# Hybrid Mamba-2 / pooling / mixture-of-experts block on one core: the table transfers of token blocks 1 to 3 wait for the mixer's last product

## What is computed

```python
x = x + (g_ssd * y_ssd + g_pool * y_pool) @ w_mix_out[i]
h = rms_norm(x, ffn_norm_g[i])
...
logits = (hf @ w_router + b_router).astype(jnp.float32)
top_val, top_idx = lax.top_k(logits, TOP_K)
weights = jax.nn.softmax(top_val, axis=-1)
...
xb = hf[tok]
gu = xb @ w_gate_up[e] + b_gate_up[e]
gate, up = jnp.split(gu, 2, axis=-1)
...
act = (up + 1.0) * gate * jax.nn.sigmoid(SWIGLU_ALPHA * gate)
return act @ w_down[e] + b_down[e]
```

## Time and profile before

| what | value |
|---|---|
| median of 3 runs | 1843.52 us |
| the profiled execution's own time | 1857.41 us |
| span in the profile, first to last instruction | 1855.6 us |
| PE busy | 1808.1 us (97%) |
| DVE busy | 1411.4 us (76%) |
| ACT busy | 1179.0 us (64%) |
| POOL busy | 363.7 us (20%) |
| mean granted clock of TensorE | 0.991 |
| mixer, up to the slot transfers | 0 to about 617 us of the span |
| experts, steady | about 675 to 1770 us of the span |

### The profile page before, as it was taken

One profiled execution on the slowest core, in us unless ns is written; L12 is line 12 of the kernel. 1 busy time (PEld: TensorE's weight loads), 2 busy tenths in 40 slices (PEclk: granted clock), 3 DMA queues, 4 the chain that ended last, 5 costly groups with the idle time before them and its releaser, 6 DMA issues.

```text
span 1855.6 us, 25522 instructions
## 1 busy us (share of the span) xinstructions
PE 1808.1 (97%) x8997; PEld 1501.0 (81%) x8997; DVE 1411.4 (76%) x1027; ACT 1179.0 (64%) x936; POOL 363.7 (20%) x324
## 2 busy tenths in 40 slices
PE   7999999999999799999999999999999999999997
PEld 6888888678889778888888888888888888888876
DVE  4576676553334489989998988988988988989974
ACT  5655565342232367777777777777777777777774
POOL 5223324520000321211221221111111211121000
PEclk9999999999999899999999999999999999999999
DMA  6434443343346189999999999999999999999941
GB/s 184 131 96 103 115 133 99 103 142 91 92 140 258 58 326 372 368 369 379 370 374 373 375 368 383 370 374 385 375 368 377 376 373 374 376 371 368 380 162 46
DMA packets 153769, 504.50 MB, mean 272 GB/s; under 512 B 15691, under 2 KB 76147, under 8 KB 120085
## 3 DMA queue, kind: packets, MB, share of 16 engines
q1 hardware_dynamic: 141684, 478.50, 68.9%
q0 software_dynamic: 11984, 25.22, 5.8%
q10 hardware_dynamic: 48, 0.07, 0.0%
HBM read 493.67 MB, written 26.30 MB: 280 GB/s over the span
## 4 chain that ended last, share of the span: by engine, by line
PE 84%; DVE 5%; ACT 3%; POOL 3%; issue 3%; DMA 1%; another core or an unknown queue 1%; SPq 0%; DVEq 0%; POOLq 0%; ACTq 0%
PE gu_ps L2112 25%; PE gu_ps L2116 12%; PE dn_ps L2127 12%; PE gu_ps L1880 7%; PE gu_ps L1882 7%; PE gu_ps L1881 7%; PE dn_ps L2133 6%; PE et_ps L2098 3%; ACT w_hi L911 1%; PE dn_ps L2283 1%; PE gu_ps L1902 1%; POOL win L814 1%; POOL dx L800 1%; PE gu_ps L2283 1%; PE gu_ps L2104 1%
## 5 line engine op out<-in xcount | busy, mean ns | idle before, releaser
L1696 DVE TENSOR_TENSOR split_l<-ring,split_h 128x2048 fp32r<-128x2048 f32 x384 | 870.1, 2292 | 94.2 <-ACT split_h L1177 91.2
L1177 ACT ACTIVATE split_h<-ring 128x2048 fp32r<-128x2048 f32 x384 | 728.9, 1916 | 145.9 <-PE gu_ps L2116 114.2
L2112 PE MATMUL gu_ps<-split_h,xgT_h 128*128 128x512 f32 x992 | 272.9, 397 | 1.5 <-DVE xgT_l L1702 1.5
L2112 PE MATMUL gu_ps<-split_h,xgT_l 128*128 128x512 f32 x992 | 266.9, 391 | 0.0
L2116 PE MATMUL gu_ps<-split_l,xgT_h 128*128 128x512 f32 x992 | 266.8, 391 | 0.0
L2116 PEld LDWEIGHTS gu_ps<-split_l,xgT_h 128*128 128x128 f32 x992 | 186.8, 188 | 40.1
L2112 PEld LDWEIGHTS gu_ps<-split_h,xgT_l 128*128 128x128 f32 x992 | 186.6, 188 | 40.1
L2112 PEld LDWEIGHTS gu_ps<-split_h,xgT_h 128*128 128x128 f32 x992 | 181.6, 188 | 43.4 <-issue 8.6
L1356 DVE TENSOR_TENSOR w_lo<-w_raw,w_hi 128x2048 fp32r<-128x2048 f32 (+1 forms) x45 | 102.8, 2285 | 143.2 <-ACT w_hi L911 130.8
L827 POOL COPY icur<-slots 128x1 int32 (+1 forms) x31 | 50.6, 1631 | 670.3 <-PE et_ps L2098 670.3
L2127 PE MATMUL dn_ps<-split_h,actT_h 128*128 128x512 f32 x496 | 155.4, 394 | 0.0
(11 more groups left out here) (358 smaller groups left out, 2625.3 us busy)
## 6 DMA issues: line engine op xcount, KB each, us to landing
ring<-in_w_gate_up SPq DMA_DIRECT2D x256, 1024.0 KB, 7.2
ring<-in_w_down SPq DMA_DIRECT2D x128, 1024.0 KB, 7.9
w_raw<-in_w_in SPq DMA_DIRECT2D x28, 1024.0 KB, 5.9
arow<-acum_rows POOLq DMA_DIRECT2D x16, 512.0 KB, 6.5
w_raw<-in_w_ssd_out SPq DMA_DIRECT2D x8, 1024.0 KB, 6.1
w_raw<-in_w_in SPq DMA_DIRECT2D x9, 512.0 KB, 6.4
w_raw<-in_w_mix_out SPq DMA_DIRECT2D x4, 1024.0 KB, 8.8
wpg<-in_w_ple_gate SPq DMA_DIRECT2D x2, 2048.0 KB, 20.1
```

The costliest lines, as they stand in the source:

```text
L1177: a.activation(split_h[s % SPLIT][:, :], ring[s % RING][:, :], ACT.Copy).then_inc(hi_done, 1)
L1696: v.tensor_tensor(split_l[s % SPLIT][:, :], ring[s % RING][:, :], split_h[s % SPLIT][:, :].bitcast(F32), ALU.subtract).then_inc(lo_done, 1)
L2112: t.matmul(gu_ps[:, b * 512:b * 512 + 512], x[:, k, :], split_h[s][:, b * 512:b * 512 + 512], start=False, stop=False)
```

## The change

After `send(0)`, GpSimd waits until VectorE has read the last product of the mixer's output, `MO(3, 1)`, and only then goes on to `send(1)`, `send(2)` and `send(3)`. Nothing else is touched.

```diff
             pool.wait_ge(filled, 16 * PASSES + 16)
-            for c in range(CH):
+            send(0)
+            wait_proj_read(pool, ("MO", CH - 1, 1))
+            for c in range(1, CH):
                 send(c)
             pool.wait_ge(rows_stored, 16 * CH)
             step(g.memset(xg[:, :], 0.0))
```

## The result

The changed kernel takes 1850.73 us (median of 6 runs, 1849.1 to 1851.91); the kernel before took 1843.32 us beside it (6 runs, 1841.73 to 1845.19). The ratio is 1.0038, with a 95% interval of 1.0028 to 1.0048: slower by 7.4 us. The forecast was 1848.3, slower by 4.8.

What follows compares the result with a forecast made beforehand. PE was taken to bound the expert stage, so a delayed start delays the end. With no stall in timed runs, 4.8 us of late transfers added to 1843.5 gave 1848.3 us; range 1835.0 to 1851.5.

Steps and rivals of the forecast that it cites:

- the forecast's case: Seam before the experts: timed runs have no stall, the hold only makes slot transfers late, 4.8 us slower; chance 0.50.
- the transfer that was to be held by the norm: POOL's block 1 and 2 transfers after the wait: one of the eight was expected to be held by VectorE's norm.
- The page rule that I weighed against the trace: Descriptor generation not seen to stall under tensor_tensor; by it the change costs the wait's 3.1 us alone, 1846.6 us.
- the sum: All lateness at the seam reaches the end and nothing later wins it back: 1843.5 + 4.8 = 1848.3 us.
- the 4.8: Lateness in us of SP's weight issue from the wait and transfers held by splits; estimates 3.7 to 7.2, mostly 4.8.
- the prediction's own baseline: Kernel before rebuilt without the stall: last row_idx 632.6, SP's weights 644.7, 1857.4 less 11.8 giving 1845.6 us.
- The reading that fell: Residual add's 9.8 us stall before the router belongs to the profiled execution, not the timed runs; held at 7 in 10.
- The gap: Profiled time less median, 13.9 us before; shrinking to 2 us in the changed kernel would confirm the no-stall reading.
- The first rival: The residual add's stall is in every run and the hold removes it: 7.0 us gained, 1836.5 us; chance 0.30.
- Its point of decision: The first rival decides if the residual add's stall in timed runs is over 4.8 us long.
- D: Expectation in the experiments: chips differ in speed alone, whatever the kernel, so the ratio is 1.004 everywhere.
- C: Expectation in the experiments: the stall belongs to a chip; ratio 0.9975 where the kernel before stands near 1855, 1.004 near 1843.

Runs made afterwards that it cites:

- e3: Kernel before with blocks 1 to 3 held until VectorE has written the last normed block (h2_done = 4): 1855.15 us, ratio 0.9996.
- e2: Kernel before with the same wait placed only ahead of send(3), where it is already met: 1855.42 us, ratio 1.0001.
- e5: The changed kernel, unchanged, beside the kernel before on the second chip: 1847.99 us, ratio 0.9974.
- e4: Kernel before without a hold, plus four more indirect transfers of block 2 into a spare table ahead of block 3: 1859.07 us, ratio 1.0026.
- e9: The kernel before, unchanged, profiled again on the third chip: 1856.15 us, ratio 1.0003.
- e7: Kernel before, with SP issuing the first expert's chunks 6 and 7 before it waits for the slot transfers: 1854.76 us, ratio 1.0007.
- e11: Kernel before, with GpSimd gathering before it weighs and SP issuing the second expert's first two chunks ahead of the biases: 1855.15 us, ratio 1.0.
- e1: The kernel before, unchanged, profiled once more on the first chip: 1854.01 us, ratio 0.9999.
- e10: The changed kernel, unchanged, on the third chip: 1848.83 us, ratio 0.9961 against the kernel before.
- e6: Kernel before with the wait placed ahead of block 2, so that block 1 goes unheld: 1850.89 us, ratio 0.9984.
- e8: Changed kernel, with SP issuing the first expert's chunks 6 and 7 before it waits for the slot transfers: 1850.72 us, ratio 0.9986 against the kernel before.

## Why the prediction was right, and where it was not

**The sign and the mechanism.** In the first comparison it went as the forecast's case said, step by step: the wait costs 2.8 us at block 1 (626.75 against 623.9, where an unheld one would follow the fourth, issued at 622.63; predicted 3.1), the add is free, `row_idx` comes 8.0 us behind the start of the add (8.1, counted from 624.5), SP issues 15.6 us after it (15 to 18), and the second expert begins at 668.72 (near 669). That delay passes on undiminished to the second expert is shown by e3. That a wait which delays nothing costs nothing is shown by e2. One small step was wrong: the transfer that was to be held by the norm is free (628.03, 0.97 us, with the norm at 627.96).

The page rule that I weighed against the trace, the Trainium skill, "SBUF — State Buffer", section "Who interferes with whom" (descriptor generation not seen to stall under tensor_tensor), does not fit this trace: four transfers of 1.90 to 2.93 us stand beside such splits, and the 1846.6 us that would follow from the rule are too few. The measurement decides.

**The size.** The term that was mis-sized is what stands behind the seam, which the sum took as untouched: "Nothing later wins it back, since PE bounds the experts". Nothing wins it back, but something adds to it. The late chunks make PE pause, and in this profile the granted clock falls behind the pause; later the second expert's first products run in half clock. In 10 of the 14 profiles the time from PE's start on that expert to its activation is about 23.1 us, in e5 for one, with the clock full. In the changed kernel's it is 25.6. So the clock takes about 2.6 us there, in this execution. If the timed runs of the kernel before lose nothing at that place, the sum is 4.8 + 2.6 = 7.4, which is what was measured. That it meets the number exactly is luck: the 4.8 is an estimate, and by the prediction's own baseline (SP at 644.7, so the second expert at 663.4) the second expert comes 5.3 us late. The same correction mends the baseline. I rebuilt it from the profile at 1845.6, and that profile carries a loss of its own there (24.7 against 23.1, 1.6 us); without it the baseline is 1844.0, within 0.7 of the 1843.3 that was timed. That the kernel before runs with the clock full there when nothing stalls is argued, not shown: no profile of it without the stall exists. e3, the other seam without a stall at the add, shows the loss as well (24.7 us), with its pauses still longer. But e4 and the first profile of the kernel before, which do stall, show 24.7 too, and e9, the same kernel as the latter, 23.1. So the cause of this loss is not settled, nor is it shown for each timed run: of the changed kernel's 6, four have the profile's mean granted clock of 0.994, and the two fastest, 1849.1 and 1849.92 us, have 0.995 and 0.996.

**The reading that fell.** I put the stall down to the profiled execution, at 7 in 10, because the profile was 13.9 us above the median. Outside the first comparison the runs speak against it: the kernel before stalls in both later profiles (9.10 and 9.08) and in those of its variants without a hold (9.05 in e2, 5.37 in e7, 9.07 in e11), profiled and other runs agree (1852.9 and 1854.0; 1857.7 and 1856.2), and the levels are those of a kernel with the stall. On the second chip the kernel before itself was timed but not profiled. By the Trainium skill, "NOTIFIC — the notification-queue block", section "7.1 Overflow: three behaviours, one of which stalls the engine", the stall could have been the profiler's. e1 and e9 do not bear that out, since the profiled run costs nothing extra there, but they don't rule it out either: every execution of the later groups, and every one of the changed kernel in the first comparison, has its span and granted clock on record, and so was recorded in some way, while the 6 executions of the kernel before at 1843.3 have only their times there. Recording alone does not bring the delay, though: the changed kernel's first profile has none. The step that failed is "So the likeliest reading is that the runs that are timed don't have this stall". It may hold for the first comparison, but one profile, of an execution that is none of the timed ones, was thin ground for it. The gap did shrink to under 2 us, as the reading asked, but it would have done so in any kernel whose add doesn't stall; that sign could not tell the readings apart.

**The first rival** was right in its sign wherever the runs have the stall: 5.1 us gained on the second chip and 7.0 on the third, against 7.0 worked out. Its point of decision, a stall of over 4.8 us, fits too: it is 9.1 us in the profiles of the first and third chip. That its price was met is luck. It had the last `row_idx` 12.4 us earlier and SP's issue 5.4 us further behind it. From block 2's `row_idx` to the last one it is 19.9 us in e9 and 13.3 in e10, so 6.5 us were won, since a wait of 5.38 us came up at the ranks; and SP issues 11.9 us behind the last `row_idx` in both, so nothing was lost there.

**What stays open** is why the first comparison's timed runs of the kernel before lie 10 to 13 us below all later ones. That the stall is missing in them is inferred from this level. Its profiles differ from all of mine in more than the stall. The first place is the write-back of the experts' rows, from 680 to 1750 us (line, count, busy us, mean ns, idle before); in the changed kernel's profile of the first comparison:

```profile
L856 POOL DMA_INDIRECT x_rows<-y_sb,dcur x30 | 60.8, 2027 | 26.6 <-POOL dcur L853 26.6
```

and in e1:

```profile
L856 POOL DMA_INDIRECT x_rows<-y_sb,dcur x30 | 111.0, 3700 | 26.6 <-POOL dcur L853 26.6
```

The same instruction takes 2.03 us there and 3.70 us in the later profiles; the first profile of the kernel before has 2.10. And 30 experts take 1052.5 us in both of the first profiles, 1050.9 in all twelve later ones. The delay at the ranks differs as well: absent in the changed kernel's first profile, 4.69 and 5.38 us in e5 and e10. So the surroundings were not the same, and D's plain difference of speed, which would be one way everywhere, doesn't cover it. But the first profile of the kernel before, with the marks of the first comparison, has the stall. Which chip that comparison ran on isn't on record. So C is not settled. I also didn't try POOL busy with other work, or direct transfers in place of indirect ones, so which part of the transfers delays PE's signal is open.

## What to carry to other kernels

Before a difference between a profile and the timed runs is called the profiler's, see whether the profiled execution is one of the timed ones, and profile the unchanged kernel again, on another chip too. Holding back transfers that nobody waits for yet costs their lateness one to one if they end up last on the way into the next stage, and the granted clock may fall with the pause; it pays only where their presence delays something by more than that. And a gain that hangs on such a delay should be timed on several chips before it is kept.

## What I had not expected of the hardware

A wait for PE can last 2 to 12 us too long while GpSimd issues indirect transfers, with PE itself going on to other work (the earlier trace rows for the matmul, for the wait). It hits VectorE, and ScalarE too (2.19 us in e3, 2.92 in e4, 3.56 in e7). VectorE's wait for ScalarE stays at 0.80 us beside such a transfer in e5, so it looks as if PE's signals alone come late; no run separates the signal from the waiting engine. At the add the delay grows with the transfers in flight: none in e3 with none, 4.64 us in e6 with block 1, 9.1 in e1 with blocks 1 and 2, 11.9 in e4 with four more, with e7 (5.37) as the exception. It can end before the transfers do, and a later wait is then hit (e4, e7); if one wait is spared, another is hit (e5, e10). Not every wait is hit: VectorE's wait for PE's router product in e5, 0.31 us up to 629.27 with three transfers issued, is short, and in the changed kernel's first profile none is long. The profile calls the releaser "remote", which is a hint that none of the recorded engines was late.

Two smaller ones: slot transfers of 1 KB each land 3.8 us behind their last issue when 1 MB loads are in flight, against 1.2 us otherwise (e8 and e5), but 1.8 in e7 with the same loads; and issuing two of the chunk loads 1.7 us earlier, against e9, moved the split that waits for them by nothing (e11).
